# Final RMSNorm and output stores of a pass deferred into the next pass of a hybrid decoder trunk (8 cores)

## The chip, the cores and the metric

One Trainium2 chip, all 8 of its NeuronCores. Each core runs the same program on its own share: one prompt sequence of 2048 tokens and 16 of the 128 sample sequences (4 tokens each). The cores do not exchange data. The metric is the device time in microseconds of the slowest core.

## The reference

One layer of a decoder trunk in float32, with D_MODEL = 1024, and then a last RMSNorm. Cut to what matters:

```
h = rmsnorm(x, g_mix)
u, q, k, v, og, zr, ga, gb = split(h @ w_in)      # 512,256,256,512,512,16,1024,1024 columns
pool_out = pool_mix(u)      # 4 channel groups, trailing windows 2/4/8/16, mean minus token, linear map
y_a = pool_out @ w_pool_proj
o   = gated linear attention(q, k, v, log_sigmoid(zr @ w_gk_up + b_gk) / 16), 4 heads
y_b = (rmsnorm(o) * silu(og)) @ w_gla_proj
x = x + (sigmoid(ga) * y_a + sigmoid(gb) * y_b) @ w_out
x = x + (silu(gate) * up) @ w_ffn_out             # gate, up = split(rmsnorm(x, g_ffn) @ w_ffn_in)
y = rmsnorm(x, g_final)
```

Sixteen learned meta tokens stand ahead of every prompt and are dropped from its output. The outputs are y for prompt and sample rows, and the pooling and attention states.

## The kernel before, in words

The tokens of a core are cut into units of 128 rows, and one unit `S` of 96 rows that holds the meta tokens and the 64 sample rows. Four passes run over them: `S,0,1,2,3`, then `4..7`, `8..11`, `12..15` (line 366). In this text they are called pass 0 to pass 3. A prompt unit of a pass has slot 0 to 3, `S` has slot 4. `xres` (128 x 5 x 1024, float32) holds the residual rows of each slot; the same slot is used again by the next pass.

All engines are programmed by a tracker (`Trk`, line 96): the order in which the Python code calls `T.op` and `T.dma` is the order of the instructions in each engine's queue. The tracker adds the semaphore waits that a read or a write of a tile needs. An engine does its instructions in that order.

A pass goes so:

- `norm1`: the rows x are loaded into `xres` by DMAs of the SP queue (lines 420 to 426). In pass 0 they are normed and transposed into `hT`. From pass 1 on, `hT` was already made by the pass before (`pf_chain`, `pf_tr`, lines 884 and 901), from a second copy of x staged in `Eb`, so `xres` is first read at the output projection (line 862).
- `in_u`: TensorE projects the pooling input (line 436, four groups of 8 matmuls). ScalarE copies each of the four results into `Eb[:, g, 15:527]` (line 460) and then the 15 columns of history ahead of it (line 463). In the last pass one more projection of unit 15 goes to `uTM` (ScalarE, line 497).
- `in_qk`: four more groups of 8 matmuls, copied out by ScalarE (line 508).
- `pool`: for each group g of four, VectorE does one add over `Eb` (line 514), g more adds (line 521) and a scale and subtract into `pooled` (line 528); TensorE applies the group's map (line 535), ScalarE copies it out (line 537).
- `in_kzr`: TensorE projects zr (line 551), VectorE copies it to `zrT` (line 554); for each unit TensorE projects k (line 447), copied out by VectorE (line 559), and multiplies `zrT` by w_gk_up (lines 562, 563), which ScalarE turns into the gate.
- `in_vog`: v (copied out by VectorE, line 575), then og (ScalarE Silu, line 584, VectorE, line 586).
- `gla` with `mrgA` in its gaps (its first matmul is line 603), `mrgB`, `wout` (lines 859, 862), `norm2`, `ffn` (lines 955, 958, 989, 992) with the next pass's `hT` made in its last third.
- `final` (lines 1002 to 1021): for each unit of the pass, ScalarE squares its 1024 columns with a sum (line 1007, the result itself goes to the scratch tile `hTM`), takes Ln (line 1009) and Exp (line 1012) of one column; VectorE multiplies the rows by the scale and `gfin_bc`, in place in `xres` (line 1015); and the SP queue stores them (lines 1019, 1021).

The weights come as slabs of up to 1 MB (in bf16) through four ring buffers. Slab j + 4 is issued on the POOL queue when slab j is released (`slab_release`), that is when its last matmul is done. Eight PSUM banks are used in turn.

The part of the program around the change is the end of a pass (`final`) and the start of the next: the loads of x, then `in_u`, `in_qk`, `pool`, `in_kzr`, `in_vog`.

Of the kernel before, what the change touches and what calls it, by code (L numbers as in the profile page):

```python
# [191 lines left out]
def build_program():  # L192
# [74 lines left out]
    T = Trk(nc, es)  # L267
# [6 lines left out]
    def bk(i):  # L274
        return ('bank', i)

    try:
# [65 lines left out]
        def slab_topup():  # L343
            while sl['issued'] < len(all_specs):
                j = sl['issued']
                if j - NRING >= 0 and not sl['done'][j - NRING]:
                    break
                i = j % NRING
                for (vf, src) in all_specs[j]:
                    T.dma('pool', f'd_ring{i}', vf(ring[i]), src, writes=[('ring', i)])  # L350
                sl['issued'] += 1

        def next_slab():
            slab_topup()
            j = sl['next']; sl['next'] += 1
            assert j < sl['issued'], "slab not issued (missing release?)"
            return j, j % NRING

        def slab_release(j):
            sl['done'][j] = True  # L360
            slab_topup()
# [4 lines left out]
        passes = [['S', 0, 1, 2, 3], [4, 5, 6, 7], [8, 9, 10, 11], [12, 13, 14, 15]]  # L366

        prefetched = False
        for pi, units in enumerate(passes):
            has_s = units[0] == 'S'  # L370
            pt = [u for u in units if u != 'S']
            uslot = {}
# [7 lines left out]
            order = (['S'] if has_s else []) + pt  # L380
            rows = {u: (SROWS if u == 'S' else 128) for u in order}
# [11 lines left out]
            def norm_a(u, gbc, gkey, ssc):  # L393
                us = uslot[u]; r = rows[u]; c0, cn = ucol[u]
                xt = xres[0:r, us, :]
                hb, hk = hb_of(u)
                T.op('act', lambda e: e.activation(out=hb[0:r, :], in_=xt, func=AF.Square, accum_out=stat[0:r, ssc:ssc + 1]),
                     reads=[('x', us)], writes=[hk, ('stat', ssc)])
                T.op('act', lambda e: e.activation(out=stat[0:r, ssc + 1:ssc + 2], in_=stat[0:r, ssc:ssc + 1], func=AF.Ln,
                                                   scale=1.0 / D, bias=EPS),  # L400
                     reads=[('stat', ssc)], writes=[('stat', ssc + 1)])
                T.op('act', lambda e: e.activation(out=stat[0:r, ssc + 2:ssc + 3], in_=stat[0:r, ssc + 1:ssc + 2], func=AF.Exp,
                                                   scale=-0.5),
                     reads=[('stat', ssc + 1)], writes=[('stat', ssc + 2)])
                T.op('dve', lambda e: e.scalar_tensor_tensor(out=hb[0:r, :], in0=xt, scalar=stat[0:r, ssc + 2:ssc + 3],
                                                             in1=gbc[0:r, :], op0=ALU.mult, op1=ALU.mult),
                     reads=[('x', us), ('stat', ssc + 2), gkey], writes=[hk])

            def norm_b(u):
                us = uslot[u]; r = rows[u]; c0, cn = ucol[u]  # L410
                hb, hk = hb_of(u)
                b = nbank()
                T.op('pe', [(lambda e, c=c: e.transpose(out=banks_b[b][:, c * 128:c * 128 + r], in_=hb[0:r, c * 128:(c + 1) * 128],
                                                         identity=ident_b[0:r, 0:r])) for c in range(8)],
                     reads=[hk, 'identb'], writes=[bk(b)])
                T.op('act', lambda e: e.activation(out=hT[:, :, c0:c0 + r],  # L416
                                                   in_=banks_b[b][:, :].rearrange("p (c n) -> p c n", c=8)[:, :, 0:r], func=AF.Copy),
                     reads=[bk(b)], writes=[('hT', uslot[u])])

            for u in order:  # L420
                us = uslot[u]
                if u == 'S':
                    T.dma('sp', f'd_x{us}', xres[0:16, us, :], meta[:, :], writes=[('x', us)])
                    T.dma('sp', f'd_x{us}', xres[32:96, us, :], xs[:, :], writes=[('x', us)])
                else:
                    T.dma('sp', f'd_x{us}', xres[:, us, :], xp[u * 128:(u + 1) * 128, :], writes=[('x', us)])
            if not prefetched:
                for u in order:
                    norm_a(u, gmix_bc, 'gmix', uslot[u] * 4)
                for u in order:  # L430
                    norm_b(u)
# [67 lines left out]
                T.dma('sp', 'd_out', pbp[:, :], uTM[113:128, :], reads=['uTM'])  # L499

            slab_release(j_u)
            T.tag = f'p{pi}_in_qk'
            j_qk, slot = next_slab()
            for blk in blocks:
# [35 lines left out]

            T.tag = f'p{pi}_in_kzr'
            slab_release(j_qk)
            j_kz, slot = next_slab()
            if pi == 0:
                for c in range(8):
# [10 lines left out]
            for u in order:  # L556
                us = uslot[u]; r = rows[u]; c0, cn = ucol[u]
# [10 lines left out]
                     reads=[('sp', us)], writes=[('sp', us)])  # L568
            T.tag = f'p{pi}_in_vog'
            slab_release(j_kz)  # L570
            j_v, slot = next_slab()
            for u in order:
                us = uslot[u]; r = rows[u]
                tm_out(slot, u, 512, lambda b: T.op(
                    'dve', lambda e: e.tensor_copy(out=vTM[0:r, us, :], in_=banks[b][0:r, :]),
                    reads=[bk(b)], writes=[('vTM', us)]))
            slab_release(j_v)
            j_og, slot = next_slab()
            for u in order:
                us = uslot[u]; r = rows[u]  # L580
# [271 lines left out]
            for u in order:  # L852
                T.tag = f'p{pi}_wout'
                us = uslot[u]; r = rows[u]
# [19 lines left out]
            nxt = passes[pi + 1] if pi + 1 < len(passes) else None  # L874
# [35 lines left out]
            for gi, (f0, nf) in enumerate(FF_GROUPS):  # L910
# [67 lines left out]
                for half in range(2):  # L978
# [5 lines left out]
                    for u in order:  # L984
                        us = uslot[u]; r = rows[u]
# [13 lines left out]
                        T.tag = f'p{pi}_ffn'  # L999
            while deferred:  # L1000
                deferred.pop(0)()
            T.tag = f'p{pi}_final'
            for u in order:
                us = uslot[u]; r = rows[u]
                ssc = 40 + us * 4
                xt = xres[0:r, us, :]
                T.op('act', lambda e: e.activation(out=hTM[0][0:r, :], in_=xt, func=AF.Square, accum_out=stat[0:r, ssc:ssc + 1]),
                     reads=[('x', us)], writes=[('hTM', 0), ('stat', ssc)])
                T.op('act', lambda e: e.activation(out=stat[0:r, ssc + 1:ssc + 2], in_=stat[0:r, ssc:ssc + 1], func=AF.Ln,
                                                   scale=1.0 / D, bias=EPS),  # L1010
                     reads=[('stat', ssc)], writes=[('stat', ssc + 1)])
                T.op('act', lambda e: e.activation(out=stat[0:r, ssc + 2:ssc + 3], in_=stat[0:r, ssc + 1:ssc + 2], func=AF.Exp,
                                                   scale=-0.5),
                     reads=[('stat', ssc + 1)], writes=[('stat', ssc + 2)])
                T.op('dve', lambda e: e.scalar_tensor_tensor(out=xt, in0=xt, scalar=stat[0:r, ssc + 2:ssc + 3],
                                                             in1=gfin_bc[0:r, :], op0=ALU.mult, op1=ALU.mult),
                     reads=[('x', us), ('stat', ssc + 2), 'gfin'], writes=[('x', us)])
                if u == 'S':
                    T.dma('sp', f'd_y{us}', y_s[:, :], xres[32:96, us, :], reads=[('x', us)])
                else:  # L1020
                    T.dma('sp', f'd_y{us}', y_p[u * 128:(u + 1) * 128, :], xt, reads=[('x', us)])
            prefetched = nxt is not None

    except StopBuild:
# [47 lines left out]
```

How the kernel before makes its waits and increments, by code:

```python
    def _wait(self, e, deps, skip=()):  # L142
        for s, v in deps.items():
            if s in skip:
                continue
            if self.waited[e].get(s, 0) < v:
                self.eng[e].wait_ge(self.sems[s], v)
                self.waited[e][s] = v
# [11 lines left out]
    def op(self, e, fns, reads=(), writes=()):  # L160
        if callable(fns):
            fns = [fns]
        self._tick()
        deps = self._deps(reads, writes)
        own = 'E_' + e
        self._wait(e, deps, skip=(own,) if e == 'pe' else ())
        ins = None
        for f in fns:
            ins = f(self.eng[e])
        self.log.append((e, self.tag, len(fns)))
        self.tot[own] += 1
        ins.then_inc(self.sems[own], 1)
        self._commit((own, self.tot[own]), reads, writes)
# [1 line left out]
    def dma(self, q, sem, out, in_, reads=(), writes=(), **kw):  # L175
        self._tick()
        self._sem(sem)
        deps = self._deps(reads, writes)
        self._wait(q, deps, skip=(sem,))
        ins = self.eng[q].dma_start(out=out, in_=in_, **kw)
        self.tot[sem] += 16
        ins.then_inc(self.sems[sem], 16)
        self._commit((sem, self.tot[sem]), reads, writes)
# [1 line left out]
    def wait_all(self, e, semnames):  # L185
        for s in semnames:
            if self.tot.get(s, 0) > 0 and self.waited[e].get(s, 0) < self.tot[s]:
                self.eng[e].wait_ge(self.sems[s], self.tot[s])
                self.waited[e][s] = self.tot[s]
```

## Time and profile before

| what | value |
|---|---|
| time, median of 2 runs | 1249.9 us (1248.46 to 1251.33) |
| time of the profiled execution | 1252.22 us |
| its span on the slowest core (core 0) | 1250.8 us |
| spans of the other cores | 1229.7 to 1246.7 us |
| mean granted TensorE clock of core 0 | 0.930 |

All trace times below are microseconds from the start of core 0's span. A line of the timeline gives the start, the busy time, the engine, the source line, the operation, the tile written, the tiles read, the shape and the number of instructions merged, and in brackets the idle time of the engine before it with what ended that. PE is TensorE's matmul queue, DVE VectorE, ACT ScalarE, POOL GpSimd, SPq the SP queue.

### The profile page before, as it was taken

The numbers are of one execution on the slowest core, as the hardware profiler recorded it, in microseconds if no ns is written. First come the engines' busy times: TensorE is split into PE (matmuls) and PEld (weight loads), VectorE is DVE, ScalarE is ACT, GpSimd is POOL, SyncE is SP. The second block draws the span as 40 slices with busy tenths as digits, with TensorE's granted clock in tenths as the row PEclk, the third lists the DMA queues.
The fourth block names the chain that finished last, engine by engine and source line by source line (L and its number), as shares of the span: only waits on it lengthen the run. The fifth ranks groups of instructions, "written<-read, shape, count | busy, mean of one in ns | idle before, by whom it ended". The sixth has DMA issues, their size and how long they took to land.

```text
span 1250.8 us, 15475 instructions; the slowest of 8 cores (1229.7 to 1250.8 us)
## 1 busy us (share of the span) xinstructions
PE 1015.3 (81%) x5093; PEld 499.2 (40%) x5184; DVE 479.8 (38%) x827; ACT 432.4 (35%) x879; POOL 127.9 (10%) x157
## 2 busy tenths in 40 slices
PE   0487668798987987787998897778997997879996
PEld 0254434343433444333444344333443454334442
DVE  2043535324242625442223636441222635432224
ACT  2332546410105425543023435542023535531102
POOL 1030001000011100011111100110111100101110
PEclk9999879898999879898999889898998998989999
DMA  8985038859688895495998995397999993896994
GB/s 200 129 109 89 1 51 131 123 84 152 118 129 150 125 227 80 74 135 90 155 141 142 156 222 88 52 144 112 148 146 152 178 167 51 107 150 86 147 138 118
DMA packets 154427, 156.33 MB, mean 125 GB/s; under 512 B 13822, under 2 KB 147727, under 8 KB 154206
## 3 DMA queue, kind: packets, MB, share of 16 engines
q0 software_dynamic: 136080, 122.96, 69.3%
q1 hardware_dynamic: 16286, 28.66, 7.4%
q10 hardware_dynamic: 1984, 3.73, 1.1%
q8 instruction: 43, 0.70, 0.2%
q14 instruction: 34, 0.28, 0.1%
HBM read 267.09 MB, written 11.40 MB: 223 GB/s over the span
## 4 chain that ended last, share of the span: by engine, by line
PE 63%; DVE 11%; DMA 10%; ACT 9%; issue 6%; DVEq 0%; ACTq 0%; POOL 0%; SPq 0%; POOLq 0%
PE ps L955 12%; PE ps L958 11%; PE ps L989 11%; PE ps L447 7%; DMA ring<-w_in 4%; DMA ring<-w_out 4%; PE ps L830 3%; PE ps L859 3%; DMA ring<-w_ffn_in 3%; PE ps L436 3%; PE ps L774 2%; DVE Sf L689 2%; PE ps L785 2%; PE ps L833 1%; PE ps L562 1%
## 5 line engine op out<-in xcount | busy, mean ns | idle before, releaser
L989 PE MATMUL ps<-ring,actb 128*128 128x512 bf16 (+1 forms) x733 | 174.3, 397 | 31.1 <-DVE actb L895 21.3
L955 PE MATMUL ps<-hT,ring 128*128 128x512 bf16 x685 | 168.6, 387 | 6.3 <-ACT hT L416 3.8
L958 PE MATMUL ps<-hT,ring 128*128 128x512 bf16 x688 | 166.2, 382 | 1.7 <-DMA ring<-w_ffn_in 0.9
L963 DVE TENSOR_TENSOR actb<-ps,sgt 128x512 bf16<-128x512 f32 x88 | 60.8, 691 | 247.7 <-PE ps L958 217.4
L961 ACT ACTIVATE sgt<-ps 128x512 f32<-128x512 f32 x88 | 52.5, 597 | 282.2 <-PE ps L955 281.4
L989 PEld LDWEIGHTS ps<-ring,actb 128*128 128x128 bf16 (+1 forms) x748 | 76.5, 104 | 124.8 <-issue 47.3
L992 DVE TENSOR_TENSOR xres<-xres,ps 128x512 f32<-128x512 f32 (+1 forms) x102 | 70.1, 687 | 113.8 <-PE ps L989 112.9
L955 PEld LDWEIGHTS ps<-hT,ring 128*128 128x128 bf16 x704 | 69.5, 99 | 90.5 <-issue 10.8
L958 PEld LDWEIGHTS ps<-hT,ring 128*128 128x128 bf16 x704 | 69.4, 99 | 86.5 <-issue 5.5
L447 PE MATMUL ps<-ring,hT 128*128 128x512 bf16 (+3 forms) x416 | 87.5, 368 | 1.1 <-issue 0.8
L180 POOL DMA_DIRECT2D ring<-w_ffn_in x48 | 42.3, 882 | 350.1 <-PE ps L989 125.7
L180 POOL DMA_DIRECT2D ring<-w_in x40 | 35.1, 884 | 416.7 <-PE ps L643 101.8
L859 PE MATMUL ps<-ring,merged 128*128 128x512 bf16 (+1 forms) x264 | 62.4, 386 | 13.1 <-DVE merged L844 9.5
L774 PE MATMUL ps<-hT,ring 128*128 128x512 bf16 (+1 forms) x317 | 71.5, 376 | 0.3 <-issue 0.2
L436 PE MATMUL ps<-hT,ring 128*128 128x512 bf16 (+1 forms) x315 | 61.2, 356 | 11.2 <-DMA ring<-w_in 10.8
L830 PE MATMUL ps<-hT,ring 128*128 128x512 bf16 (+1 forms) x315 | 67.2, 358 | 0.4 <-issue 0.2
L447 PEld LDWEIGHTS ps<-ring,hT 128*128 128x128 bf16 (+1 forms) x424 | 42.9, 105 | 47.1 <-issue 15.1
L711 PE MATMUL ps<-ident_b,ofb 128*128 128x128 bf16 (+1 forms) x68 | 8.0, 255 | 53.9 <-DVE ofb L705 53.9
L436 PEld LDWEIGHTS ps<-hT,ring 128*128 128x128 bf16 x320 | 29.1, 103 | 41.9 <-issue 13.0
L788 DVE TENSOR_TENSOR merged<-ps,sgt 128x512 bf16<-128x512 f32 (+1 forms) x40 | 24.2, 604 | 54.2 <-ACT sgt L782 49.2
L859 PEld LDWEIGHTS ps<-ring,merged 128*128 128x128 bf16 (+1 forms) x272 | 26.6, 101 | 44.7 <-issue 17.6
L774 PEld LDWEIGHTS ps<-hT,ring 128*128 128x128 bf16 x320 | 31.3, 110 | 31.1 <-issue 8.6
(163 smaller groups left out, 1192.1 us busy)
## 6 DMA issues: line engine op xcount, KB each, us to landing
ring<-w_ffn_in POOLq DMA_DIRECT2D x40, 1024.0 KB, 12.8
ring<-w_in POOLq DMA_DIRECT2D x32, 1024.0 KB, 13.6
ring<-w_ffn_out POOLq DMA_DIRECT2D x16, 1024.0 KB, 12.3
xres<-xp SPq DMA_DIRECT2D x16, 512.0 KB, 11.1
ring<-w_out POOLq DMA_DIRECT2D x8, 1024.0 KB, 13.0
y_p<-xres SPq DMA_DIRECT2D x16, 512.0 KB, 10.6
Eb<-xp SPq DMA_DIRECT2D x12, 512.0 KB, 7.8
ring<-w_ffn_out POOLq DMA_DIRECT2D x8, 768.0 KB, 9.8
```

The costliest lines, as they stand in the source:

```text
L180: ins = self.eng[q].dma_start(out=out, in_=in_, **kw)
L436: T.op('pe', [(lambda e, k=k: e.matmul(banks[b][:, 0:cn], lhsT=ring[slot][:, k, wcol0:wcol0 + 128], rhs=hT[:, k, c0:c0 + cn], start=(k == ...
L447: T.op('pe', [(lambda e, k=k: e.matmul(banks[b][0:r, 0:ncols], lhsT=src[:, k, c0:c0 + r], rhs=ring[slot][:, k, wc0:wc0 + ncols], start=(k ...
L774: T.op('pe', [(lambda e, k=k: e.matmul(banks[ba][:, 0:cn], lhsT=ring[sga][:, k, j * 128:(j + 1) * 128], rhs=hT[:, k, c0:c0 + cn], start=(k ...
L830: T.op('pe', [(lambda e, k=k: e.matmul(banks[bb_][:, 0:cn], lhsT=ring[sgb][:, k, j * 128:(j + 1) * 128], rhs=hT[:, k, c0:c0 + cn], start=( ...
L859: T.op('pe', [(lambda e, k=k: e.matmul(banks[b][0:r, :], lhsT=merged[:, k, c0:c0 + r], rhs=ring[slot][:, k, :], start=(k == 0), stop=(k == ...
L955: T.op('pe', [(lambda e, k=k: e.matmul(banks[bg][:, 0:cn], lhsT=ring[sg][:, k, j * 128:(j + 1) * 128], rhs=hT[:, k, c0:c0 + cn], start=(k ...
L958: T.op('pe', [(lambda e, k=k: e.matmul(banks[bu_][:, 0:cn], lhsT=ring[su][:, k, j * 128:(j + 1) * 128], rhs=hT[:, k, c0:c0 + cn], start=(k ...
L961: T.op('act', lambda e: e.activation(out=sgt[ti][:, 0:cn], in_=banks[bg][:, 0:cn], func=AF.Silu), reads=[bk(bg)], writes=[('sgt', ti)])
L963: T.op('dve', lambda e: e.tensor_tensor(out=actb[:, sub + j, c0:c0 + cn], in0=banks[bu_][:, 0:cn], in1=sgt[ti][:, 0:cn], op=ALU.mult), rea ...
L989: T.op('pe', [(lambda e, k=k: e.matmul(banks[b][0:r, :], lhsT=actb[:, k, c0:c0 + r], rhs=ring[slot][:, k, :], start=(k == 0), stop=(k == n ...
L992: T.op('dve', lambda e: e.tensor_tensor(out=xres[0:r, us, half * 512:(half + 1) * 512], in0=xres[0:r, us, half * 512:(half + 1) * 512], in ...
```

## The change

The last RMSNorm and the stores of passes 0 to 2 are no longer written at the pass's end. They are collected, `S` first, and called in the next pass at four places: two units after `in_u` and ahead of `in_qk`, one ahead of `in_kzr`, one ahead of `in_vog`, and what is left between v and og. The load of x into a slot is issued after one of these calls, in the same queue (SP) as the stores. The last pass does its final norms at once, as before.

```diff
         prefetched = False
+        pending_fin = []
         for pi, units in enumerate(passes):
...
-            for u in order:
+            def load_x_unit(u):
                 us = uslot[u]
...
                     T.dma('sp', f'd_x{us}', xres[:, us, :], xp[u * 128:(u + 1) * 128, :], writes=[('x', us)])
+            xq = list(order)
+
+            def drain_fin(n):
+                for _ in range(n):
+                    if not pending_fin:
+                        break
+                    pending_fin.pop(0)()
+                    if len(pending_fin) < len(xq):
+                        load_x_unit(xq.pop(0))
+                if not pending_fin:
+                    while xq:
+                        load_x_unit(xq.pop(0))
+            if not pending_fin:
+                drain_fin(0)
...
             slab_release(j_u)
+            drain_fin(2)
             T.tag = f'p{pi}_in_qk'
...
             T.tag = f'p{pi}_in_kzr'
             slab_release(j_qk)
+            drain_fin(1)
             j_kz, slot = next_slab()
...
             T.tag = f'p{pi}_in_vog'
             slab_release(j_kz)
+            drain_fin(1)
             j_v, slot = next_slab()
...
             slab_release(j_v)
+            drain_fin(9)
             j_og, slot = next_slab()
...
-            T.tag = f'p{pi}_final'
-            for u in order:
-                us = uslot[u]; r = rows[u]
+            def final_unit(u, us, r, pi_):
+                T.tag = f'p{pi_}_final'
                 ssc = 40 + us * 4
...
+            fins = [(lambda u=u, us=uslot[u], r=rows[u], pi_=pi: final_unit(u, us, r, pi_)) for u in order]
+            if nxt is None:
+                for f_ in fins:
+                    f_()
+            else:
+                fins_sorted = [f for f, u in zip(fins, order) if u == 'S'] + [f for f, u in zip(fins, order) if u != 'S']
+                pending_fin.extend(fins_sorted)
```

## Rows read from the trace of the kernel before

**Rows 1.** The profile page: its head, busy time by engine, chain that ended last
```profile
span 1250.8 us, 15475 instructions; the slowest of 8 cores (1229.7 to 1250.8 us)
PE 1015.3 (81%) x5093; PEld 499.2 (40%) x5184; DVE 479.8 (38%) x827; ACT 432.4 (35%) x879; POOL 127.9 (10%) x157
PE 63%; DVE 11%; DMA 10%; ACT 9%; issue 6%; DVEq 0%; ACTq 0%; POOL 0%; SPq 0%; POOLq 0%
```

**Rows 2.** Timeline, from pass 1 to pass 2
```profile
691.69 4.42 PE L989 MATMUL ps<-ring,actb 128*128 128x512 bf16 x10 [7.23 <-DVE actb L895]
...
704.11 1.04 ACT L1007 ACTIVATE hTM<-xres 128x1024 bf16<-128x1024 f32 x1
...
705.23 13.98 PE L436 MATMUL ps<-hT,ring 128*128 128x512 bf16 x63
...
705.63 0.20 ACT L1012 ACTIVATE stat<-stat 128x1 f32<-128x1 f32 x1
705.74 1.04 ACT L1007 ACTIVATE hTM<-xres 128x1024 bf16<-128x1024 f32 x1
...
706.17 4.87 DVE L1015 SCALAR_TENSOR_TENSOR xres<-xres,stat,gfin_bc 128x1024 f32<-128x1024 f32 x4
...
707.53 3.96 SPq L180 DMA_DIRECT2D y_p<-xres  x4
...
710.96 0.70 DVE L514 TENSOR_TENSOR sgt<-Eb 128x526 f32<-128x526 f32 x1
...
713.14 0.21 ACT L463 ACTIVATE Eb<-Ehist 128x15 f32<-128x15 f32 x1
...
717.38 6.95 SPq L180 DMA_DIRECT2D xres<-xp  x4
...
722.18 0.38 PE L535 MATMUL ps<-pooled,wpg_b 128*128 128x512 bf16 x1 [2.33 <-ACT Ehist L532]
...
722.65 0.69 ACT L537 ACTIVATE pool_out<-ps,pscale_c 128x512 bf16<-128x512 f32 x1 [0.61 <-PE ps L535]
...
725.42 0.66 PE L562 MATMUL ps<-wgk_s,zrT 16*128 16x256 f32 x2
...
749.62 0.38 PE L603 MATMUL ps<-cs,spT 128*128 128x128 f32 x2
```

**Rows 3.** Groups of instructions of the whole run: the final scaling (count, busy, mean ns)
```profile
L1015 DVE SCALAR_TENSOR_TENSOR xres<-xres,stat,gfin_bc 128x1024 f32<-128x1024 f32 (+1 forms) x17 | 20.8, 1279 | 0.5 <-ACT stat L1012 0.5
```

**Rows 4.** Timeline, from pass 0 to pass 1
```profile
431.30 0.70 DVE L514 TENSOR_TENSOR sgt<-Eb 128x526 f32<-128x526 f32 x1
...
432.28 0.21 ACT L463 ACTIVATE Eb<-Ehist 128x15 f32<-128x15 f32 x1
...
442.52 0.38 PE L535 MATMUL ps<-pooled,wpg_b 128*128 128x512 bf16 x1 [3.52 <-DVE pooled L528]
...
473.10 0.38 PE L603 MATMUL ps<-cs,spT 128*128 128x128 f32 x2
```

**Rows 5.** Timeline, from pass 2 to pass 3
```profile
985.01 0.70 DVE L514 TENSOR_TENSOR sgt<-Eb 128x526 f32<-128x526 f32 x1
...
988.23 0.60 ACT L497 ACTIVATE uTM<-ps 128x512 f32<-128x512 f32 x1 [0.82 <-PE ps L447]
...
996.24 0.38 PE L535 MATMUL ps<-pooled,wpg_b 128*128 128x512 bf16 x1 [0.60 <-DVE pooled L528]
...
1022.13 0.38 PE L603 MATMUL ps<-cs,spT 128*128 128x128 f32 x2
```

**Rows 6.** Stretches: length, TensorE busy (count), granted clock, DMA share, GB/s
```profile
443.00:447.00 4.00, 4.00 (x16) 0.60 1.04 198
...
691.00:696.00 5.00, 4.31 (x10) 0.50 1.24 192
```

**Rows 7.** Timeline, output projection of pass 1 and its two slabs
```profile
534.04 1.76 POOL L180 DMA_DIRECT2D ring<-w_out  x2 [10.52 <-PE ps L830]
...
551.18 5.34 PE L859 MATMUL ps<-ring,merged 128*128 128x512 bf16 x24 [1.40 <-DMA ring<-w_out]
```

## Prediction, made before the changed kernel was run

> **What bounds the kernel now.** I read the page first. TensorE is busy 81% of the span and holds 63% of the chain of waits that ended last; VectorE holds 11%, DMA 10% and ScalarE 9% of it [rows 1]. So the spine is TensorE, and what counts is where it stands still. The change touches the start of passes 1, 2 and 3, so I then read the timeline there, engine by engine.
>
> What the reader is to see in it: TensorE doesn't wait for the final norms. In pass 2 it starts the first projection at 705.23 and goes through 64 matmuls in 13.98 us, while ScalarE still squares (704.11, 705.74) and VectorE still scales (706.17, four instructions in 4.87 us) [rows 2]. The norms cost TensorE nothing there. What they delay is VectorE's pooling chain: its first instruction (L514) starts at 710.96, right behind the last L1015 [rows 2]. The chain's last result lets TensorE go on with the fourth L535, and there it has stood still: 3.52 us in pass 1, 2.33 in pass 2, 0.60 in pass 3 [rows 2, 4, 5]. From the first L514 to that L535 it is 722.18 - 710.96 = 11.22 us, and 11.22 and 11.23 in the other two [rows 2, 4, 5]: VectorE works without a gap, and the chain is as long as its own work. When it starts decides when TensorE goes on.
>
> **What the change removes.** At the end of passes 0 to 2 the final norms go: 5 + 4 + 4 = 13 squares, as many L1015 of 1.28 us [rows 3] and as many stores. None was on TensorE's path, as shown. The most that can be won is what follows from an earlier pooling chain, and that is small: the three stalls, 3.52 + 2.33 + 0.60 = 6.45 us.
>
> **What it adds ahead of the pooling chain.** The first call, two units, is written after the first projection and before `in_qk` and `pool`. So in ScalarE's queue two squares stand behind the last copy into `Eb` (in pass 3 behind L497), and in VectorE's queue two L1015 stand ahead of the first L514, though `Eb` is ready. Queued behind them: on ScalarE the four qk copies, on VectorE the whole pooling chain, and for that TensorE waits.
>
> The price of a unit: from a square's start to the end of its Exp 705.63 + 0.20 - 704.11 = 1.72 us; the next square starts 1.63 us after the first; each L1015 takes 1.28 [rows 2, 3]. In pass 2 the last copy of history starts at 713.14 and takes 0.21. The first square can start at 713.45 (0.1 between instructions), the second at 715.1, its scale is there at 716.8, the second L1015 runs from 716.9 to 718.2, and the pooling chain starts at 718.2 in place of 710.96 [rows 2]: 7.2 us late. In general it starts 5.1 us after the last L463, or 5.5 after L497, which is 0.4 longer. Pass 1: 432.28 + 5.1 = 437.4 for 431.30, 6.1 us late [rows 4]. Pass 3: 988.23 + 5.5 = 993.7 for 985.01, 8.7 us late [rows 5]. In all three TensorE already waits at the fourth L535, so nothing hides it: **6.1 + 7.2 + 8.7 = 22.0 us**, and the stalls become 9.6, 9.5 and 9.3 us. The four qk copies on ScalarE are about 3.3 us late (two squares of 1.63); TensorE has eight PSUM banks and then stands at the pooling chain anyway, so I put them at nothing; without that cover they would cost at most those 3.3 us a pass.
>
> **The third unit, ahead of `in_kzr`.** ScalarE takes the square behind the last L537 (722.65 + 0.69), so its scale is there 1.72 us later, about 725.1; L1015 runs to 726.5; only then comes the copy of zr, about 0.7 long, and L562 could start at 727.5 in place of 725.42 [rows 2]. That is 2.1 us if TensorE's clock is full. If the clock is low, L551 and L447 ahead of it take longer and hide this.
>
> **TensorE's clock behind the longer stall.** In pass 2, an idle time of 7.23 us ahead of L989 is followed by a stretch in which the granted clock is 0.50, the 1.2 GHz level [rows 2, 6]. Behind the 3.52 us of pass 1 it is 0.60 over 443 to 447 [rows 4, 6]. The stretch from the fourth L535 to L603, the same work each time, takes 473.10 - 442.52 = 30.58 us in pass 1, 27.44 in pass 2 and 25.89 in pass 3: the longer the stall ahead of it (3.52, 2.33, 0.60), the slower [rows 2, 4, 5]. The changed kernel has 9.3 us or more ahead of each. I take pass 1's 30.6 for all three, with the wait for zr lying under the low clock: 0 + 3.1 + 4.7 = **7.8 us**. The low end: the clock is as good as in pass 3 and only the zr wait is added, 28.0 three times, -2.6 + 0.6 + 2.1 = 0.1 us. The high end: pass 1's 30.6, the zr wait on top (2.1) and another slow stretch like that of 691 to 696, which loses 2.5 us of its 5.0: 7.8 + 3 x 4.6 = 21.6. I take the value near pass 1, since its stall is the nearest row.
>
> The Trainium skill (TensorE: Matmul & The Clock Gate, section "Part 1: The HAM clock gate") says that the array falls from 2.4 to 1.2 GHz once it has been idle, and comes back only after sustained work. Rows 6 agree. By that rule alone each of the three stalls would be followed by one slow stretch such as the 5.0 us one, a loss of 2.5 us each, 7.5 us in all less what pass 1 already pays; the sum above by whole stretches says 7.8.
>
> **What else is moved.** The fourth unit (and pass 1's fifth) falls beside the v and og projections, where ScalarE waits for TensorE; vTM copies move by under 1.3 us, with eight banks for them: nothing. The SP queue: today four stores go out from 707.53 and the loads of x start at 717.38, when the first store has landed, 9.9 us on [rows 2]. After the change every load stands ahead of the next store and waits for the store before: four rounds of some 11 us, so in pass 1 the last load goes out near 437 + 44 = 481 and lands before 500. `xres` is needed at the output projection, whose matmuls run at 551 [rows 7]: hidden, with 50 us to spare. No other work is queued on SP then. On POOL nothing moves but by TensorE's delay.
>
> **Sum.** 22.0 + 7.8 = 29.8 us on the profiled execution, 1252.2 to 1282.0. That execution stands 2.3 us above the median, so the median goes from 1249.9 to **1279.7**, 2.4% slower. Two per cent of this kernel, 25 us, is about what a measurement tells from no change, so the sign of the verdict hangs on the second term.
>
> **Rivals.**
> *The stall alone.* The chain is late by 22.0 us, but the clock adds little (the low end, 0 to 3 us): 1249.9 + 22 to 25 = 1272 to 1274.9, within 2%. For it: pass 3 has hardly a slow stretch; against it: pass 1 has, behind a stall a third as long.
> *More than the forecast.* Clock and zr wait add up: 15 to 21.6 us (the high end) on top of 22.0, so 1287 to 1293.5. Against it: the two lie on the same microseconds.
> *The other side.* What the change says comes true: ScalarE's copies into `Eb` are no longer behind the squares, the pooling chain starts when the first group is there, a quarter of the four groups' 7.0 us (13.98 / 2) and the copies' 0.6 + 0.2 and two gaps behind TensorE's start: about 2.8 us, at 708.0 in pass 2 in place of 710.96, and ends before TensorE needs it. Then the stalls go, -6.45, and the stretches behind them come down to pass 3's 25.89, -4.7 - 1.6: 1249.9 - 12.7 = 1237.2, faster by 1%. It decides only if the two L1015 run behind the first L514; by the order in which the calls are written they stand ahead of it, in the same queue.
> *The delay is taken up later.* TensorE's 22 us would be covered if it waited later for a transfer that doesn't move with it. It does wait for a slab at 551.18, 1.40 us, but that slab was issued at 534.04 behind TensorE's own matmuls L830 [rows 7], so it moves too. 1250 to 1262.
>
> **Chances.** Forecast 0.62, its own range 1275 to 1287. More than that 0.10. The stall alone 0.17. Taken up later 0.04. The other side 0.05. Other gains 0.02. Slower by over 2%: 0.62 + 0.10 = 0.72; within 2%: 0.17 + 0.04 + 0.05 = 0.26; faster by over 2%: 0.02. The range of 8 in 10 takes in the forecast, the stall alone and most of the higher case: 1270 to 1290.
>
> **What would show it.** Right: in the timeline of the changed kernel two L1015 directly ahead of the first L514 of passes 1 to 3, idle until ScalarE's Exp; in pass 2 L514 some 13 us behind TensorE's first matmul (718.2 - 705.2; it is 5.7 us now); idle 9 to 10 us ahead of the fourth L535, ended by `pooled`; a clock of 0.5 to 0.6 right behind; 30 to 31 us from there to L603. Wrong: L514 ahead of the L1015, no stall above 4 us, or a stretch to L603 near 26 us (then the second term falls); or TensorE waiting less for slabs later by as much as it lost here.

## The result, and the profile after

The changed kernel takes 1281.2 us in the median, where the kernel before takes 1252.4: the ratio is 1.0226, with a 95% interval of 1.019 to 1.0261. It is slower, by 28 to 29 us; 29.8 were forecast. (Now and then one die runs at a lower clock and the time is some per cent longer, with either kernel; such runs are left out of every number here, and with them the two medians are 1283.5 and 1253.1, from which the expectations below start.)

Of the page of the changed kernel, its head, the busy time and the line of the chain that ended last, which answer to [rows 1]:

```profile
span 1276.7 us, 15545 instructions; the slowest of 8 cores (1250.1 to 1276.7 us)
...
PE 1038.5 (81%) x5184; PEld 504.5 (40%) x5184; DVE 480.3 (38%) x827; ACT 433.0 (34%) x879; POOL 128.2 (10%) x157
...
PE 64%; DVE 12%; ACT 9%; DMA 9%; issue 5%; DVEq 0%; ACTq 0%; POOL 0%; SPq 0%; POOLq 0%
```

The page hides the change: the shares move by a point, and VectorE, ScalarE and GpSimd are busy as long as before, within 1 us. (TensorE has 23 us more, but 91 of its matmul records are missing in the trace before: x5093 there, x5184 here.) The reader who stops here sees nothing. The timeline from pass 1 to pass 2, on the slowest core (core 4), answers to [rows 2]. In the changed kernel the lines have new numbers: the first projection is L451, the history copies L478, the square, Exp and scaling L1025, L1030 and L1033, the pooling chain L530 to L544, the pooling matmuls L551, the zr projection L568, its use L579, the first attention matmul L622.

```profile
710.80 13.98 PE L451 MATMUL ps<-hT,ring 128*128 128x512 bf16 x64
...
713.53 0.22 ACT L478 ACTIVATE Eb<-Ehist 128x15 f32<-128x15 f32 x1
...
718.71 0.21 ACT L478 ACTIVATE Eb<-Ehist 128x15 f32<-128x15 f32 x1
718.83 1.04 ACT L1025 ACTIVATE hTM<-xres 128x1024 bf16<-128x1024 f32 x1
...
720.66 1.29 DVE L1033 SCALAR_TENSOR_TENSOR xres<-xres,stat,gfin_bc 128x1024 f32<-128x1024 f32 x1 [8.83 <-ACT stat L1030]
...
722.28 1.28 DVE L1033 SCALAR_TENSOR_TENSOR xres<-xres,stat,gfin_bc 128x1024 f32<-128x1024 f32 x1 [0.34 <-ACT stat L1030]
723.49 0.70 DVE L530 TENSOR_TENSOR sgt<-Eb 128x526 f32<-128x526 f32 x1
...
725.24 0.38 PE L551 MATMUL ps<-pooled,wpg_b 128*128 128x512 bf16 x1 [0.47 <-DVE pooled L544]
...
727.67 0.38 PE L551 MATMUL ps<-pooled,wpg_b 128*128 128x512 bf16 x1 [2.05 <-DVE pooled L544]
...
730.69 0.58 PE L551 MATMUL ps<-pooled,wpg_b 128*128 128x512 bf16 x1 [2.65 <-DVE pooled L544]
730.86 0.33 SPq L180 DMA_DIRECT2D xres<-xp  x1
731.28 0.52 SPq L180 DMA_DIRECT2D y_p<-xres  x1
...
734.71 0.59 PE L551 MATMUL ps<-pooled,wpg_b 128*128 128x512 bf16 x1 [3.43 <-DVE pooled L544]
735.23 3.58 PE L568 MATMUL ps<-hT,ring 128*16 128x512 bf16 x8
...
739.94 0.67 PE L579 MATMUL ps<-wgk_s,zrT 16*128 16x256 f32 x2
...
754.97 0.33 SPq L180 DMA_DIRECT2D xres<-xp  x1
...
760.91 0.39 PE L622 MATMUL ps<-cs,spT 128*128 128x128 f32 x2
```

Read it by queue. VectorE has its first group of `Eb` at 713.8, but its next instruction is an L1033, and that waits 8.83 us for the scale, because ScalarE squares only behind its last copy. Both L1033 done, L530 starts at 723.49, 12.69 us behind TensorE's first matmul where it was 5.73. TensorE is through its 64 matmuls and then waits four times for `pooled`: 0.47 + 2.05 + 2.65 + 3.43 = 8.60 us.

The other two passes look the same. The view of the pooling matmuls alone gives the idle time of TensorE before them and how often, over the whole run; one wait of 2.48 us in pass 0 is in it, with either kernel. Before, it was three waits of 6.6 us by VectorE and one of 2.3 put down to ScalarE (the 2.33 us of pass 2), so 6.45 us in passes 1 to 3. After, on core 4:

```profile
  DVE pooled L544: 27.9, 12
```

That is 25.4 us in passes 1 to 3.

The clock behind the stall, by stretches of the same core, which answers to [rows 6] (length, TensorE busy and count, granted clock, DMA share, GB/s):

```profile
711.00:725.00 14.00, 13.78 (x64) 1.00 1.24 135
725.00:734.00 9.00, 1.34 (x3) 0.70 1.14 198
734.00:738.50 4.50, 3.79 (x9) 0.50 0.98 292
738.50:742.00 3.50, 3.39 (x22) 0.95 0.43 82
742.00:762.00 20.00, 20.00 (x100) 1.00 0.75 177
```

TensorE stands almost idle over 725 to 734, and over the next 4.5 us its clock is 0.50, the 1.2 GHz level: L568 takes 3.58 us for eight matmuls.

All eight cores, read from their timelines in the same way (us; the mean of eight cores; chain and matmul are counted from TensorE's first matmul of the pass):

| | pass 1 before / after | pass 2 | pass 3 |
|---|---|---|---|
| pooling chain starts | 6.92 / 12.69 | 5.73 / 12.69 | 5.73 / 14.11 |
| fourth pooling matmul | 18.16 / 23.93 | 16.96 / 23.91 | 16.96 / 25.34 |
| from there to the first attention matmul | 28.89 / 29.71 | 26.43 / 26.37 | 25.29 / 26.89 |

The first two rows spread by less than 0.1 us over the cores, the third by up to 5.5 us. The fourth pooling matmul is 5.77 + 6.95 + 8.38 = 21.1 us late.

### The profile page after: what moved, and what is told of

Read it like the earlier page. It is cut to its first block, busy times and chain, and to the rows that moved or that the text cites. A ratio compares the mean times of both kernels' runs of the same rounds, so it can differ in the third digit from the quotient of the medians.

```text
span 1276.7 us, 15545 instructions; the slowest of 8 cores (1250.1 to 1276.7 us)
## 1 busy us (share of the span) xinstructions
PE 1038.5 (81%) x5184; PEld 504.5 (40%) x5184; DVE 480.3 (38%) x827; ACT 433.0 (34%) x879; POOL 128.2 (10%) x157
## 4 chain that ended last, share of the span: by engine, by line
PE 64%; DVE 12%; ACT 9%; DMA 9%; issue 5%; DVEq 0%; ACTq 0%; POOL 0%; SPq 0%; POOLq 0%
PE ps L974 12%; PE ps L977 11%; PE ps L1008 11%; PE ps L462 7%; PE ps L878 4%; PE ps L849 3%; DMA ring<-w_in 3%; DMA ring<-w_out 3%; DMA ring<-w_ffn_in 3%; PE ps L451 3%; DVE Sf L708 2%; PE ps L793 1%; PE ps L852 1%; DVE sgt L537 1%; PE ps L804 1%
## 5 line engine op out<-in xcount | busy, mean ns | idle before, releaser
L1008 PE MATMUL ps<-ring,actb 128*128 128x512 bf16 (+1 forms) x748 | 169.6, 387 | 29.8 <-DVE actb L914 21.3
L974 PE MATMUL ps<-hT,ring 128*128 128x512 bf16 x704 | 171.3, 387 | 5.8 <-ACT hT L417 3.8
L977 PE MATMUL ps<-hT,ring 128*128 128x512 bf16 x704 | 169.8, 385 | 1.0 <-DMA ring<-w_ffn_in 1.0
L462 PE MATMUL ps<-ring,hT 128*128 128x512 bf16 (+3 forms) x424 | 91.5, 378 | 0.0
L878 PE MATMUL ps<-ring,merged 128*128 128x512 bf16 (+1 forms) x272 | 67.7, 408 | 12.6 <-DVE merged L863 9.9
L451 PE MATMUL ps<-hT,ring 128*128 128x512 bf16 (+1 forms) x320 | 61.5, 357 | 6.4 <-DMA ring<-w_in 6.4
L462 PEld LDWEIGHTS ps<-ring,hT 128*128 128x128 bf16 (+1 forms) x424 | 44.2, 109 | 49.5 <-issue 16.3
L807 DVE TENSOR_TENSOR merged<-ps,sgt 128x512 bf16<-128x512 f32 (+1 forms) x40 | 24.2, 604 | 53.2 <-ACT sgt L801 48.0
L451 PEld LDWEIGHTS ps<-hT,ring 128*128 128x128 bf16 x320 | 29.2, 103 | 37.4 <-issue 8.5
```

What stands on the lines that cost most here:

```text
L451: T.op('pe', [(lambda e, k=k: e.matmul(banks[b][:, 0:cn], lhsT=ring[slot][:, k, wcol0:wcol0 + 128], rhs=hT[:, k, c0:c0 + cn], start=(k == ...
L462: T.op('pe', [(lambda e, k=k: e.matmul(banks[b][0:r, 0:ncols], lhsT=src[:, k, c0:c0 + r], rhs=ring[slot][:, k, wc0:wc0 + ncols], start=(k ...
L878: T.op('pe', [(lambda e, k=k: e.matmul(banks[b][0:r, :], lhsT=merged[:, k, c0:c0 + r], rhs=ring[slot][:, k, :], start=(k == 0), stop=(k == ...
L974: T.op('pe', [(lambda e, k=k: e.matmul(banks[bg][:, 0:cn], lhsT=ring[sg][:, k, j * 128:(j + 1) * 128], rhs=hT[:, k, c0:c0 + cn], start=(k ...
L977: T.op('pe', [(lambda e, k=k: e.matmul(banks[bu_][:, 0:cn], lhsT=ring[su][:, k, j * 128:(j + 1) * 128], rhs=hT[:, k, c0:c0 + cn], start=(k ...
L1008: T.op('pe', [(lambda e, k=k: e.matmul(banks[b][0:r, :], lhsT=actb[:, k, c0:c0 + r], rhs=ring[slot][:, k, :], start=(k == 0), stop=(k == n ...
```

## The experiments

Theory A: what costs is the place of the two L1015 (now L1033) in VectorE's queue, ahead of the pooling chain, and through it TensorE's stall. Rival B: it is ScalarE, whose squares hold up its copies. Rival C: it is the deferring of the stores and loads, through SP's order or the traffic. Theory D: the clock behind the stall is part of the loss. The ratios below are to the kernel before, run on the same chip; "mean of cores" is the mean span of the eight cores over the runs, which the luck of the slowest core moves less. All other times and views are of one execution of each kernel. The mean of cores is 1239.6 and 1239.5 us for the kernel before in the two sets of runs, and 1267.4 for the changed kernel.

**All norms at v and og.**

```diff
             slab_release(j_u)
-            drain_fin(2)
...
             slab_release(j_qk)
-            drain_fin(1)
...
             slab_release(j_kz)
-            drain_fin(1)
+            drain_fin(2)
```

> Edit: the changed kernel with its first two calls taken out; two units are called ahead of in_vog and the rest between v and og. Theory A (the two L1015 ahead of the pooling chain in VectorE's queue are the cost): the chain starts 2.8 us behind TensorE's first matmul of the pass (12.7 us in the changed kernel, 5.7 to 6.9 before), the fourth pooling matmul runs 14.7 us behind it (16.4 in pass 3) in place of 23.9 and 25.4, the stretch from there to the first attention matmul is 24.2 to 25.7 us; the time is 1253 - 10 = 1243, faster than before by 0.8%. Rival C (deferring the stores and loads itself costs, by the SP queue's serial order or by traffic): the loss stays for the most part, 1265 or more. Rival D (late clock): chain early but the stretches stay at 28 to 31 us, about 1250.

Measured: 1241.8 us, ratio 0.992 (0.9896 to 0.9944), faster than both kernels. Mean of cores 1230.5. Its timeline at the start of pass 1 (core 0; the pooling chain is L529 to L543 here, its matmul L550, the scaling L1031):

```profile
420.34 13.98 PE L451 MATMUL ps<-hT,ring 128*128 128x512 bf16 x63
...
423.38 0.71 DVE L529 TENSOR_TENSOR sgt<-Eb 128x526 f32<-128x526 f32 x1 [2.02 <-ACT Eb L478]
...
433.86 0.69 DVE L543 SCALAR_TENSOR_TENSOR pooled<-sgt,Eb 128x512 bf16<-128x512 f32 x1
434.15 1.07 PE L550 MATMUL ps<-pooled,wpg_b 128*128 128x512 bf16 x4
...
449.69 1.28 DVE L1031 SCALAR_TENSOR_TENSOR xres<-xres,stat,gfin_bc 96x1024 f32<-96x1024 f32 x1 [4.20 <-ACT stat L1028]
```

The chain starts 3.04 us behind TensorE's first matmul, and the four pooling matmuls run as one group with no idle time in front. The same norms, stores and loads are deferred here, even further; so deferring as such doesn't cost, and rival C falls. The expectation of the stretch behind, 24.2 to 25.7 us, held only in part: with no stall ahead of it, it is 24.2 in 13 of the 24 core-passes (24.86 counted from the first of the merged four matmuls, 0.65 earlier), but 27.5 to 30.7 in the others, above all in pass 3.

**Only the squares ahead of qk.** As the last, but the ScalarE part of two units (square, Ln, Exp; `pending_sq`) stays where the change has it:

```diff
             slab_release(j_u)
+            for sq_ in pending_sq:
+                sq_()
...
-            def final_unit(u, us, r, pi_):
-                T.tag = f'p{pi_}_final'
+            def final_sq(us, r):
...
+            def final_unit(u, us, r, pi_, squared=False):
...
+                if not squared:
+                    final_sq(us, r)
...
+                pending_sq = [(lambda us=uslot[u], r=rows[u]: final_sq(us, r)) for u in srt[:2]]
```

> Edit: as e1, but the squares, Ln and Exp of the first two units stand ahead of the qk projection on ScalarE, as in the changed kernel; their scaling on VectorE and their stores stay at v and og. Theory A: ScalarE's part costs nothing, the pooling chain starts 2.8 us behind TensorE's first matmul, the time is that of e1 within 2 us (1243 to 1245). Rival B (the squares on ScalarE, which hold up the qk copies and the history copies, are the cost): fourth pooling matmul at 18 us or later, time 1265 to 1283.

Measured: 1244.7 us, ratio 0.995 (0.9931 to 0.9969), mean of cores 1233.4. Its timeline in pass 1 (core 0; square L1026, chain L533 to L547, matmul L554):

```profile
432.58 12.68 PE L452 MATMUL ps<-hT,ring 128*128 128x512 bf16 x57
...
435.63 0.71 DVE L533 TENSOR_TENSOR sgt<-Eb 128x526 f32<-128x526 f32 x1 [2.02 <-ACT Eb L479]
...
440.62 1.04 ACT L1026 ACTIVATE hTM<-xres 96x1024 bf16<-96x1024 f32 x1
...
443.87 1.66 ACT L527 ACTIVATE qkT<-ps 128x512 f32<-128x512 f32 x3
...
446.40 1.11 PE L554 MATMUL ps<-pooled,wpg_b 128*128 128x512 bf16 x4
```

The two squares stand in the same place as in the changed kernel, the qk copies are as late and run three in a row, and the chain and TensorE are where they were without the squares (the group of four matmuls starts 13.8 us behind the first matmul of the pass in both). Of some 39 us between the fastest kernel and the changed one, the squares bring back 2.9, in the median as in the mean of cores, and the two intervals overlap. Rival B falls, which expected 1265 to 1283; A holds. Whether the 2.9 us are real, and where they come from, isn't shown: the chain and the fourth matmul don't move, and the three stretches behind sum up to 78.1 us in the mean of cores against 77.7. ScalarE isn't without a part in the changed kernel, though: the L1033 waits for its squares, as the next experiment shows.

**The dose: one unit ahead of qk, and all of them.**

```diff
             slab_release(j_u)
-            drain_fin(2)
+            drain_fin(1)
...
             slab_release(j_qk)
-            drain_fin(1)
...
             slab_release(j_kz)
-            drain_fin(1)
+            drain_fin(2)
```

In the other kernel the first call is `drain_fin(9)` and the one ahead of in_kzr is taken out; the later ones find nothing left to do.

> Edit: the changed kernel with one unit ahead of qk in place of two, none ahead of in_kzr, two ahead of v, the rest between v and og. Theory A, by dose: the chain starts 1.63 us earlier than with two units, at 11.1 us (12.5 in pass 3), fourth pooling matmul at 22.3 (23.7); with the zr wait gone the time is 1283.5 - 3 x 1.63 - 6 = 1272.6. If the stall's length sets the clock behind it (theory D), a stall of 7 us in place of 8.6 shows the same slow stretches, 26 to 31 us.

> Edit: the changed kernel with all units (five in pass 1, four in passes 2 and 3) ahead of qk. Theory A, by dose: each further unit starts the chain 1.63 us later: 12.7 + 4.9 = 17.6 us behind TensorE's first matmul in pass 1, 16.0 in pass 2, 17.4 in pass 3; by the chain alone 1253.1 - 1251.6 aside, the two-unit time 1281 + 4.9 + 3.3 + 3.3 = 1292.5. If the qk copies, now five squares late on ScalarE, count as well (theory B), the fourth pooling matmul still follows the chain's start by 11.2 us and nothing is added; B would show it later than that. Clock (theory D): if the loss behind the stall grew with its length, the stretch to the first attention matmul would be longer than in the two-unit kernel in all passes; if only its presence counts, it stays 26 to 32.

Measured: one unit 1270.2 us (ratio 1.0154, 1.012 to 1.0187), all units 1292.0 us (1.0305, 1.0262 to 1.0348). The chain starts 11.06, 11.06 and 12.47 us behind TensorE's first matmul with one unit, 17.57, 15.94 and 17.36 with all; both as forecast to 0.1 us. VectorE's queue in pass 1 of the kernel with all units (core 1; scaling L1032, chain from L530):

```profile
438.04 1.28 DVE L1032 SCALAR_TENSOR_TENSOR xres<-xres,stat,gfin_bc 96x1024 f32<-96x1024 f32 x1 [8.83 <-ACT stat L1029]
439.66 1.28 DVE L1032 SCALAR_TENSOR_TENSOR xres<-xres,stat,gfin_bc 128x1024 f32<-128x1024 f32 x1 [0.35 <-ACT stat L1029]
...
445.75 0.70 DVE L530 TENSOR_TENSOR sgt<-Eb 128x526 f32<-128x526 f32 x1
```

The idle 8.83 us is the wait of the first unit until ScalarE comes to it, the same in either kernel. Some 2.0 us of it VectorE would wait anyway, for the first copy into `Eb` (2.02 in the kernel with all norms at v and og); with the 1.28 of the L1032 itself the first unit delays the chain by 11.06 - 3.05 = 8.0 us. A further unit costs 1.63, ScalarE's pace, not VectorE's 1.28. So the first unit ahead of the chain is by far the dearest. Against the kernel with all norms at v and og the mean of cores is 29.6 us longer with one unit, 36.9 with two and 46.2 with all.

The times fit less well than the chain. The 1272.6 us expected for one unit held a gain of 6 us from the zr wait that the next experiment doesn't find, so that it came within 3 us of the measured time is in part luck. In the mean of cores, one unit is 7.3 us faster than two where the chain gives 4.9, and all units are 9.3 slower where it gives 11.4. The clock behind the stall doesn't explain this by the stall's length: the sum of the three stretches is 84.7 us in the mean of cores with one unit (stalls of 6.8 to 7.4 us), 83.0 with two, 84.4 with all (11.1 to 13.1 us).

**No unit ahead of the zr copy.**

```diff
             slab_release(j_qk)
-            drain_fin(1)
```

> Edit: the changed kernel without the call ahead of in_kzr (two units ahead of qk, one ahead of v, the rest between v and og). Theory A: chain start stays at 12.7 us (14.1 in pass 3); the copy of zr no longer stands behind an L1015, so the fast stretch from the fourth pooling matmul to the first attention matmul falls from 26.2 to 24.2 us in each pass: 1283.5 - 6 = 1277.5. Rival (that wait is hidden under something else): stretch stays 26.2, time 1283.

Measured: 1279.6 us, ratio 1.0219 (1.0182 to 1.0257), mean of cores 1267.7 against 1267.4: no gain of 6 us. My expectation missed, and the rival in it holds. The stretch to the first attention matmul doesn't fall to 24.2 us on any core in any pass; it is 26.0 to 26.5 in pass 2 and 25.5 to 33.1 in the others. TensorE in pass 1 (core 7; zr projection L567, its use L578):

```profile
455.50 0.59 PE L551 MATMUL ps<-pooled,wpg_b 128*128 128x512 bf16 x1 [3.43 <-DVE pooled L544]
456.02 3.58 PE L567 MATMUL ps<-hT,ring 128*16 128x512 bf16 x8
459.53 1.63 PE L462 MATMUL ps<-ring,hT 128*128 128x256 bf16 x8
461.09 0.69 PE L578 MATMUL ps<-wgk_s,zrT 16*128 16x256 f32 x2
```

L567 and L462 run at the low clock and take 3.58 + 1.63 us. The copy of zr ends at 460.39, 0.7 us before TensorE wants it. In pass 2 of the changed kernel, with the unit ahead of it, the L1033 runs from 737.82 to 739.10 while L568 still runs until 738.81, and the copy ends at 739.69, still 0.25 us before L579. From the fourth pooling matmul to the use of zr it is 5.59 us here and 739.94 - 734.71 = 5.23 there. The low clock covers this wait, narrowly, as the prediction had it; the expectation of this run had forgotten it.

**The loads alone.** The kernel before, with its loads of x moved:

```diff
-            for u in order:
-                us = uslot[u]
+            def load_x():
+                for u in order:
...
+            if not prefetched:
+                load_x()
...
             slab_release(j_og)
+            if prefetched:
+                load_x()
```

> Edit: the kernel before, in which the loads of x of passes 1 to 3 are issued behind the og projection and not at the pass's start; the norms and stores stay where they were. Theory A: the SP queue's part of the change costs and gains nothing, the time is that of before within 3 us (ratio 0.998 to 1.002). Rival C (the loads and stores share the DMA engines with the weight slabs, so spreading them is what the change wins or loses): 5 us or more to either side.

Measured: 1257.3 against 1252.2 us, ratio 1.0018 (0.9979 to 1.0056), mean of cores 1241.7 against 1239.5: no change that can be told from none.

**The stall by itself.** To the kernel with all norms at v and og, seven products of constants are added ahead of the pooling chain. They are idle work and change no output.

```diff
             T.tag = f'p{pi}_pool'
+            if pi > 0:
+                for _ in range(7):
+                    T.op('dve', lambda e: e.scalar_tensor_tensor(out=hTM[0][:, :], in0=gfin_bc[:, :], scalar=1.0, in1=gffn_bc[:, :],
+                                                                 op0=ALU.mult, op1=ALU.mult),
+                         reads=[('E', 0), 'gfin', 'gffn'], writes=[('hTM', 0)])
```

> Edit: the kernel with all norms at v and og (ratio 0.992) with seven idle products of two constant tiles (128x1024, written to the scratch tile, about 1.25 us each, waiting for the first copy into Eb) ahead of the pooling chain in VectorE's queue in passes 1 to 3. No norm, store or load is moved, ScalarE and SP are untouched. Theory A with the clock term: the chain starts 3.05 + 8.8 = 11.9 us behind TensorE's first matmul, TensorE stalls some 8.3 us in each pass, 25 us in all, and the clock behind it costs 4 to 8 us more: 1241.8 + 29 to 33 = 1271 to 1275. Rival (the clock takes nothing, the rest of the changed kernel's loss is from the norms themselves): 1241.8 + 25 = 1266 to 1268.

Measured: 1273.7 us, ratio 1.0169 (1.0108 to 1.0229), mean of cores 1260.9, 30.4 more than without the seven. Start of pass 2 on core 0 (chain from L534, matmul L555, zr L571), and the clock of the stretch behind:

```profile
714.10 9.21 DVE L528 SCALAR_TENSOR_TENSOR hTM<-gfin_bc,gffn_bc 128x1024 bf16<-128x1024 f32 x7 [1.72 <-ACT Eb L475]
723.23 0.70 DVE L534 TENSOR_TENSOR sgt<-Eb 128x526 f32<-128x526 f32 x1
...
734.44 0.59 PE L555 MATMUL ps<-pooled,wpg_b 128*128 128x512 bf16 x1 [3.43 <-DVE pooled L548]
734.96 3.58 PE L571 MATMUL ps<-hT,ring 128*16 128x512 bf16 x8
```

```profile
735.00:738.00 3.00, 3.00 (x9) 0.50 0.00 0
```

No norm stands near, and the picture is that of the changed kernel. The fourth pooling matmul is at 23.09 us in all passes, where it was at 14.46, 14.46 and 16.19: 8.63 + 8.63 + 6.90 = 24.2 us. Another 6.2 us of the 30.4 come behind that. The time alone doesn't show them, for the interval of the ratio is some 7.6 us to either side and takes in the rival's 1266 to 1268. The traces do: the stretch from the fourth pooling matmul to the first attention matmul has its least value at 26.3 us over the 24 core-passes, against 24.2 without a stall, so 2.1 us for each stall at the low clock, three times 6.3; and the sum of the three stretches rises from 77.7 to 83.4 us in the mean of cores, by 5.7. So 30.4 of the 36.9 us between the kernel with all norms at v and og and the changed one are made by a stall alone, without a single norm moved near it; the fourth pooling matmul is 3.9 us less late than in the changed kernel, summed over the three passes, and that is most of the rest.

## Why the prediction was right

- *TensorE doesn't wait for the norms today, only VectorE's pooling chain does.* Right. With the norms out of its way the chain starts at 3.05 us and the three stalls are gone: 6.45 us were forecast as the most to be won from the stalls, 12.7 with the clock; the kernel that does it is 9.6 us faster in the median and 9.1 in the mean of cores.
- *Two units ahead of the chain: 6.1 + 7.2 + 8.7 = 22.0 us.* Measured 5.77 + 6.95 + 8.38 = 21.1. Each is 0.3 us less: the square starts 0.12 us behind the start of the last history copy (718.71, 718.83), where I had counted 0.3. The stall is 8.60 us and not 9.5, and it doesn't stand ahead of the fourth matmul alone, as I had looked for: it is spread over all four, which run one by one between the waits (3.43 us ahead of the fourth).
- *The qk copies cost nothing.* In the kernel with the squares alone they are as late, and the fourth pooling matmul doesn't move. The 2.9 us by which that kernel is slower are within the noise of the two ratios.
- *The zr wait lies under the low clock.* In the changed kernel 0.7 us of it is seen in pass 3 of core 7 (L579 idle 0.68 for `zrT`), and without it nothing is won. Right. Whether more of it would appear if the stall were mended and the unit left there wasn't tested.
- *The clock: pass 1's 30.6 us for all three, 7.8 us.* The size nearly came out, the reason given for it didn't, so this term was in part luck. By the prediction's own sign (a stretch near 26 us, then the second term falls) it fell in 18 of the 24 core-passes of the changed kernel, which take 26.2 to 26.9 us; only the other six take 31 us or more. I had read three rows of one core (30.58, 27.44, 25.89 behind stalls of 3.52, 2.33, 0.60) as a law. All eight cores show otherwise: the kernel before has 25.7 to 30.6 in pass 1 behind one and the same stall of 3.5; the changed kernel has 26.2 to 26.5 on all cores in pass 2 behind 8.60 us; the kernel with all units has 26.0 to 26.3 in pass 1 behind 13.1 us, its longest; and the kernel with no stall has stretches of 27.5 to 30.7. What a stall of 6.3 us or more does is leave the granted clock at 0.50 for 2.8 to 6.0 us from the fourth matmul on, on every core in every pass, about 2 us lost (the least stretch behind one is 26.2 us in the changed kernel and 25.5 in any, against 24.2). Above that, the clock goes to 0.50 a second time later in the stretch or it doesn't. With such stalls it does in 52 of 120 core-passes of five kernels, and those stretches take 28.7 to 33.1 us, the others at most 26.9; in the two kernels without a stall it does in 21 of 48, so not less often. Pass 1's 30.58 us before, from which I had the term, had this second time in it. On the slowest core the sum of the three went from 83.9 to 89.4, 5.5 us, in the mean of the eight cores from 80.6 to 83.0, 2.4. Over nine runs the mean span rises by 27.8 us, 6.7 more than the chain's 21.1, so the profiled run, whose mean is only 1262.1, was a lucky one. How much of the 6.7 lies in these stretches and how much later in the pass isn't shown.
- *SP's serial order is hidden.* Right: a load, then the next store 0.4 us behind it, and the last load of pass 2 goes out at 754.97, that of pass 1 at 481.74. The rounds of 11 us aren't there: in pass 1 of core 4 a load goes out 2.7 to 8.2 us behind the store before it. The output projection of pass 1 still finds its slab last and not its rows:

```profile
555.99 6.30 PE L878 MATMUL ps<-ring,merged 128*128 128x512 bf16 x24 [0.30 <-DMA ring<-w_out]
```

- *Nothing takes the delay up later.* Right: the mean span rises by more than the chain's delay, not less.

Against the rule of the Trainium skill (TensorE: Matmul & The Clock Gate, "Part 1: The HAM clock gate"), that idleness brings 1.2 GHz and only work brings 2.4 back: the runs agree at each stall of 6.3 us or more. The price by the one row I had used, 2.5 us for each, was near the 2.1 measured. But the clock falls without idle time too, where small matmuls follow one another (the last section has the rows), and there the measurement decides.

## What to carry to other kernels

Deferred work is not free because its engine has time: it must be written behind what the next stage waits for, in the queue on which that wait hangs. Here that was VectorE's; two squares in the same place on ScalarE moved nothing that TensorE waits for. Two instructions a pass, 1.28 us each, cost 28 us, and the same ones some stages later win 10; look for the first instruction of the next stage's chain in each queue, and ask what the one ahead of it waits for. The queue pays for the wait of a deferred instruction (8.83 us here, 6.8 of them on top of the wait that was there anyway), not only for its length (1.28).

Read a clock effect on all cores before taking it for a rule: three rows of one core fitted a law that twenty-four didn't have.

## What the runs showed of the hardware that was not expected

The stretch behind a stall loses about 2 us at half clock, and about the same behind 6.3 and 13.1 us of idle time (26.3 and 26.0 us at the least, against 24.2). And in the stage of small matmuls the granted clock falls to 0.50 while the engine is busy, with no stall ahead of it. In pass 3 of the kernel with all norms at v and og, on core 0 (k projection L462; between its groups stand the small float32 products of zr, L577 and L578):

```profile
963.00:986.00 23.00, 22.88 (x110) 1.00 1.10 134
986.00:994.00 8.00, 7.89 (x26) 0.50 0.42 69
```

```profile
984.12 1.05 PE L462 MATMUL ps<-ring,hT 128*128 128x256 bf16 x8
...
986.18 1.89 PE L462 MATMUL ps<-ring,hT 128*128 128x256 bf16 x8
```

TensorE is busy for nearly all of both stretches, and in the second the same eight matmuls take 1.89 us in place of 1.05. Why the clock falls there isn't shown. Which cores and passes it hits differs from core to core and from kernel to kernel; the metric takes the slowest core, so it stands 11 to 13 us above the mean core in either kernel (1250.2 against 1239.6 before, 1279.9 against 1267.4 after).
